# A decoder layer kernel: the gates' sigmoid by exponentials and logarithms, the suffix sums in two rounded passes

## The reference

```python
h = rms_norm(x, g_norm_mix[l]) * (1 + scale1) + shift1
proj = h @ w_in[l]                                  # q, k, v of both attention branches
...
# stick-breaking attention, 4 heads of 64
z = jnp.einsum('bqhd,bshd->bhqs', qb, kf) * scale
log_1m = jnp.where(mask, jax.nn.log_sigmoid(-z), 0.0)
suffix = lax.cumsum(log_1m, axis=3, reverse=True)
between = jnp.concatenate([suffix[..., 1:], jnp.zeros_like(suffix[..., :1])], axis=-1)
a = jnp.where(mask, jnp.exp(jax.nn.log_sigmoid(z) + between), 0.0)
...
g_dil, g_sb = jnp.split(jax.nn.sigmoid(h @ w_branch_gate[l]), 2, axis=-1)
merged = g_dil * (o_dil @ w_branch_dil[l]) + g_sb * (o_sb @ w_branch_sb[l])
x = x + gate1 * (merged @ w_out[l])
h2 = rms_norm(x, g_norm_ffn[l]) * (1 + scale2) + shift2
# 32 SwiGLU experts of width 512, two for each token; x + gate2 * y is the output
```

## Time and profile before

| | us |
|---|---|
| median of 3 runs | 959.87 |
| lowest and highest | 957.65, 960.79 |
| the profiled execution | 957.36 |
| its span in the profile | 955.6 |

### The profile page before, as it was taken

The page is one execution under the profiler, slowest core; times in us unless marked ns, Lnnn a source line. Parts: engine busy times, 40 slices in busy tenths (PEclk is TensorE's granted clock), DMA queues, the critical chain, the costliest instruction groups (busy, mean ns, idle before and its releaser), DMA issues.

```text
span 955.6 us, 11365 instructions
## 1 busy us (share of the span) xinstructions
PE 898.8 (94%) x4241; PEld 518.9 (54%) x4241; DVE 464.6 (49%) x829; ACT 197.5 (21%) x331; POOL 135.0 (14%) x168
## 2 busy tenths in 40 slices
PE   3989999999989999999899999999999999899897
PEld 2556779998867666488544443444344433333332
DVE  2441356538797766733663443344334424334224
ACT  3432233335433333403200000000000000000000
POOL 1000112302242111522101000000000000000000
PEclk9989999999999999999899999999999999999999
DMA  9966765240323203352889999999999999999995
GB/s 344 329 231 230 265 221 177 103 161 7 117 71 123 88 1 142 140 237 105 346 315 395 423 421 420 421 421 421 421 421 422 422 421 422 421 421 424 421 415 205
DMA packets 60077, 275.04 MB, mean 288 GB/s; under 512 B 8756, under 2 KB 21052, under 8 KB 31876
## 3 DMA queue, kind: packets, MB, share of 16 engines
q1 hardware_dynamic: 54772, 264.41, 69.3%
q0 software_dynamic: 3952, 9.19, 2.6%
q10 hardware_dynamic: 1312, 0.87, 0.4%
HBM read 263.71 MB, written 14.70 MB: 291 GB/s over the span
## 4 chain that ended last, share of the span: by engine, by line
PE 68%; SPq 19%; DMA 6%; DVE 3%; issue 2%; ACT 2%; DVEq 0%; ACTq 0%
PE ps L719 26%; PE ps L1093 14%; SPq L440 14%; PE ps L1112 7%; PE ps L1066 4%; DMA arena<-in_w_expert_down 3%; SPq L448 2%; PE ps L669 2%; PE ps L880 2%; SPq L395 2%; DMA arena<-in_w_ada 1%; PE ps L913 1%; PE ps L905 1%; PE ps L834 1%; DMA xn<-in_w_ada 1%
## 5 line engine op out<-in xcount | busy, mean ns | idle before, releaser
L1093 PE MATMUL ps<-arena,hT 128*64 128x512 f32 x1024 | 229.0, 596 | 5.0 <-DMA arena<-in_w_expert_up 4.4
L1093 PEld LDWEIGHTS ps<-arena,hT 128*64 128x64 f32 x1024 | 70.2, 137 | 146.7 <-issue 133.5
L1112 PE MATMUL ps<-arena,hT 128*64 128x512 f32 x512 | 116.9, 598 | 11.8 <-DMA arena<-in_w_expert_down 11.8
L1994 DVE TENSOR_SCALAR hT<-hT 128x256 f32<-128x256 f32 x32 | 9.4, 293 | 240.1 <-ACT hT L1472 240.1
L719 PE MATMUL ps<-slot_r,xs_r 128*128 128x512 f32 x320 | 106.2, 404 | 0.4 <-issue 0.4
L719 PE MATMUL ps<-xs_r,slot_r 128*128 128x512 f32 x320 | 101.8, 399 | 0.8 <-DVE hT_r L1574 0.5
L719 PE MATMUL ps<-slot_r,hT_r 128*128 128x512 f32 x224 | 88.1, 393 | 0.0
L719 PEld LDWEIGHTS ps<-slot_r,xs_r 128*128 128x128 f32 x320 | 77.3, 262 | 10.5 <-ACT arena L1332 2.5
L1112 PEld LDWEIGHTS ps<-arena,hT 128*64 128x64 f32 x512 | 33.9, 136 | 74.8 <-issue 59.6
L719 PEld LDWEIGHTS ps<-xs_r,slot_r 128*128 128x128 f32 x320 | 59.3, 190 | 16.7 <-issue 2.9
L635 POOL COPY idx<-small 128x1 int32 (+1 forms) x32 | 6.8, 212 | 414.4 <-DVE hT L2016 393.2
(11 more groups left out here) (297 smaller groups left out, 1078.1 us busy)
## 6 DMA issues: line engine op xcount, KB each, us to landing
arena<-in_w_expert_gate SPq DMA_DIRECT2D x64, 1024.0 KB, 24.5
arena<-in_w_expert_up SPq DMA_DIRECT2D x64, 1024.0 KB, 26.9
arena<-in_w_expert_down SPq DMA_DIRECT2D x32, 2048.0 KB, 29.6
xn<-in_w_ada SPq DMA_DIRECT2D x16, 1024.0 KB, 4.7
arena<-in_w_in SPq DMA_DIRECT2D x12, 1024.0 KB, 8.0
arena<-in_w_ada SPq DMA_DIRECT2D x8, 1024.0 KB, 14.6
arena<-in_w_branch_gate SPq DMA_DIRECT2D x4, 2048.0 KB, 8.1
xs<-in_x SPq DMA_DIRECT2D x8, 512.0 KB, 9.3
```

Source lines behind the costliest of these rows:

```text
L1093: mm = pe.matmul(ps[64 * h:64 * h + 64, 2, :], xeT[:, xb, k, CAP * j:CAP * (j + 1)], w_gu(b)[:, :, k, 256 * h:256 * h + 256], start=(k == ...
L1112: mm = pe.matmul(ps[64 * h:64 * h + 64, 4, :], hhT[:, f % 2, 64 * (f // 2):64 * (f // 2) + 64], w_dn(b)[:, f, h * CH:(h + 1) * CH], start= ...
```

## The change

The diff has five parts.

- Gates. Scalar takes log(1+exp(-|x|)) in three passes (`gate_log`: absolute value, exponential, logarithm), VectorE takes min(x,0) minus it out of the PSUM bank (`gate_finish`, which signals `gate_arg`), Scalar takes the exponential (`gate_close`). Gate products and branch products wait on `gate_arg` in place of `gate_exp`.
- Suffix sums. Softplus is split into a rounded part (Scalar, `split_sp`) and the rest (VectorE, `split_sp`), and the sums are 20 float32r matmuls in place of ten fp32 ones.
- adaLN. `ada_more` comes one unit later, `mod_round`, `columns` and the third bias load too.
- Tail. The two parts of x1 are first copied into natural order (Scalar, `natural`, eight copies into two free weight slots), `residual` reads them without a stride, and the middle of the last gate and up product waits for them (`hotT_ok` 5 in place of 3). `add_y` sums in place, and the output is stored from there.
- `ones` and `tri` get rounded copies, made by Scalar at the start; elsewhere `one` is the same memory as fp32.

```diff
+        ones_r = sb("ones_r", [P, P], F32R)
+        tri_r = sb("tri_r", [P, P], F32R)
...
+        sp_hi, sp_lo = (xn_r[:].rearrange("p t n -> p (t n)")[:, at:at + SB_COLS] for at in (1280, 2560))
+        one = ones_r[:].bitcast(F32)
...
-        x1n = arena[:, EXP_W:EXP_W + NT * D].rearrange("p (t n) -> p t n", t=NT)
+        x1_part = [slot_r[j][:].rearrange("p k n -> p (k n)").rearrange("p (t n) -> p t n", t=NT) for j in (3, 7)]
...
             for u in range(QK_FIRST, QK_LAST + 1):
                 m, t, ch = u - QK_FIRST, u % NT, u // NT
-                if m == 0:
+                if m == 1:
                     columns(0)
-                if m == KC + 1:
+                if m == KC + 2:
                     columns(1)
...
-            for u in range(2):
-                ada_more(u)
+            ada_more(0)
...
-                if u < 2 * KC:
-                    ada_more(u)
+                if u <= 2 * KC:
+                    ada_more(u - 1)
...
-                    pe.wait_ge(gate_exp, f)
+                    pe.wait_ge(gate_arg, f)
                 elif f >= 2:
-                    pe.wait_ge(gate_exp, f - 1)
+                    pe.wait_ge(gate_arg, f - 1)
...
                 b = 3 * (h % 2)
-                pe.wait_ge(sp_ok, h + 1)
-                for j in range(NT):
+                def sums(part, j):
                     for j2 in range(j, NT):
                         a = b * CH + SB_OFF[j] + (j2 - j) * P
-                        mm = pe.matmul(psf[:, a:a + SEQ - j2 * P], (tri if j2 == j else ones)[:],
-                                       sp_[:, SB_OFF[j2]:SB_OFF[j2] + SEQ - j2 * P],
-                                       start=(j2 == j), stop=(j2 == NT - 1), skip_group_check=True)
+                        mm = pe.matmul(psf[:, a:a + SEQ - j2 * P], (tri_r if j2 == j else ones_r)[:],
+                                       part[:, SB_OFF[j2]:SB_OFF[j2] + SEQ - j2 * P],
+                                       start=(part is sp_hi and j2 == j), stop=(part is sp_lo and j2 == NT - 1),
+                                       skip_group_check=True)
+                    return mm
+
+                pe.wait_ge(sphi_ok, h + 1)
+                for j in range(NT - 1):
+                    sums(sp_hi, j)
+                pe.wait_ge(sp_ok, 2 * h + 2)
+                for j in range(NT - 1):
+                    sums(sp_lo, j)
+                sums(sp_hi, NT - 1)
+                mm = sums(sp_lo, NT - 1)
                 mm.then_inc(sf_ps, 1)
 
...
-                    pe.wait_ge(gate_exp, 10)
+                    pe.wait_ge(gate_arg, 10)
                 elif f == 6:
-                    pe.wait_ge(gate_exp, 2 * KC)
+                    pe.wait_ge(gate_arg, 2 * KC)
...
-                            pe.wait_ge(hotT_ok, 3)
+                            pe.wait_ge(hotT_ok, 5)
...
                 for t, h in parts:
-                    bank = ps[:, final_bank(t, h), :].rearrange("p (c k) -> p c k", k=KC)
-                    for part in (xs_r, xn_r):
-                        pe.matmul(bank, ident_r[:], part[:, t, :].rearrange("p (k c) -> p c k", k=KC)[:, 64 * h:64 * h + 64, :],
-                                  start=(part is xs_r), stop=False, skip_group_check=True)
+                    for part in (0, 1):
+                        pe.matmul(ps[:, final_bank(t, h), :], ident_r[:], x1_part[part][:, t, h * CH:(h + 1) * CH],
+                                  start=(part == 0), stop=False, skip_group_check=True)
...
+            act.wait_ge(consts, 4)
+            act.activation(ones_r[:], ones[:], ACT.Copy).then_inc(consts, 1)
+            act.activation(tri_r[:], tri[:], ACT.Copy).then_inc(consts, 1)
...
-                if u == KC + 1:
+                if u == KC + 2:
...
-            def gate_exp_(f):
+            def gate_log(f):
+
                 act.wait_ge(gate_ps, f + 1)
-                act.activation(gT[:, f, :], ps[:, gate_bank(f), :], ACT.Exp, scale=-1.0).then_inc(gate_exp, 1)
+                g = gT[:, f, :]
+                link(act.activation(g, ps[:, gate_bank(f), :], ACT.Abs))
+                link(act.activation(g, g, ACT.Exp, scale=-1.0))
+                act.activation(g, g, ACT.Ln, bias=1.0).then_inc(gate_exp, 1)
+
+            def gate_close(f):
+                act.wait_ge(gate_arg, f + 1)
+                act.activation(gT[:, f, :], gT[:, f, :], ACT.Exp).then_inc(gate_ok, 1)
...
-                gate_exp_(s)
                 probs_store(s)
+                gate_log(s)
                 if s % NT in (1, 2):
                     split_hi(7 + s // NT, s % NT - 1)
                 if s >= NT + 1:
                     mix_exp(s - NT - 1)
-            gate_exp_(8)
+                if s >= 1:
+                    gate_close(s - 1)
             mix_exp(NT - 1)
+            gate_log(8)
 
...
+            def split_sp(h):
+                act.wait_ge(sp_ok, 2 * h + 1)
+                act.activation(sp_hi, sp_[:, 0:SB_COLS], ACT.Copy).then_inc(sphi_ok, 1)
 
...
-            gate_exp_(9)
+            gate_log(9)
+            split_sp(0)
+            gate_close(7)
+            gate_close(8)
             for h in range(NH):
                 if h == 0:
                     split_hi(9, 0)
                     split_hi(9, 1)
                 sb_exp(h)
+                if h == NH - 1:
+                    gate_close(15)
                 if h + 1 < NH:
                     sb_logs(h + 1)
-                    gate_exp_(10 + 2 * h)
+                    gate_log(10 + 2 * h)
+                    gate_close(9 + 2 * h)
+                    split_sp(h + 1)
+                sb_store(h)
                 if h in (1, 2):
                     split_hi(10, h - 1)
-                sb_store(h)
                 if h + 1 < NH:
-                    gate_exp_(11 + 2 * h)
+                    gate_log(11 + 2 * h)
+                    gate_close(10 + 2 * h)
...
+            def natural(part, src):
+
+                for t in range(NT):
+                    ins = act.activation(x1_part[part][:, t, :].rearrange("p (c k) -> p c k", k=KC),
+                                         src[:, t, :].bitcast(F32).rearrange("p (k c) -> p c k", k=KC), ACT.Copy)
+                ins.then_inc(hotT_ok, 1)
+
+            act.activation(ident_r[:], ident[:], ACT.Copy).then_inc(hotT_ok, 1)
+            natural(0, xs_r)
             sig(NE - 2)
-            act.activation(ident_r[:], ident[:], ACT.Copy).then_inc(hotT_ok, 1)
             for j in range(2):
                 act.wait_ge(last_ps, j + 1)
                 act.activation(hotT[:, j].rearrange("p t n -> p (t n)"), ps[:, 6 * j, :], ACT.Copy).then_inc(hotT_ok, 1)
+            natural(1, xn_r)
             sig(NE - 1)
 
             def act_round(rnd):
...
+                if u in (KC, 2 * KC):
+                    mod_round(u // KC)
...
-                if u == KC - 1:
-                    mod_round(1)
-                if u == 2 * KC - 1:
-                    mod_round(2)
-                if u == 2 * KC + 3:
+                if u == 2 * KC + 5:
...
                 dve.wait_ge(gate_exp, f + 1)
-                link(dve.tensor_scalar(gT[:, f, :], gT[:, f, :], 1.0, None, ALU.add))
-                dve.reciprocal(gT[:, f, :], gT[:, f, :]).then_inc(gate_ok, 1)
+                dve.scalar_tensor_tensor(out=gT[:, f, :], in0=ps[:, gate_bank(f), :], scalar=0.0, in1=gT[:, f, :],
+                                         op0=ALU.min, op1=ALU.subtract).then_inc(gate_arg, 1)
...
-                if s < 2 * NT - 1:
-                    gate_finish(s)
+                gate_finish(s)
...
+            def split_sp(h):
+                dve.wait_ge(sphi_ok, h + 1)
+                dve.tensor_tensor(sp_lo, sp_[:, 0:SB_COLS], sp_hi.bitcast(F32), ALU.subtract).then_inc(sp_ok, 1)
...
             sb_softplus(0)
+            split_sp(0)
             out_T(2)
             out_T(3)
-            gate_finish(2 * NT - 1)
+            gate_finish(8)
             for h in range(NH):
                 sb_args(h)
-                for f in (8, 9):
-                    gate_finish(2 * h + f)
+                gate_finish(9 + 2 * h)
                 if h < NH - 1:
                     dil_gate(2 * h)
                 if h + 1 < NH:
                     sb_copy(h + 1)
                     sb_softplus(h + 1)
+                    gate_finish(10 + 2 * h)
+                    split_sp(h + 1)
                     dil_gate(2 * h + 1)
             dil_gate(6)
             dil_gate(7)
...
-                step(dve.tensor_tensor(x1n[:, t, :], y_in[:, t, 0, :], y_in[:, t, 1, :], ALU.add))
+                step(dve.tensor_tensor(y_in[:, t, 0, :], y_in[:, t, 0, :], y_in[:, t, 1, :], ALU.add))
```

More of the change, by code:

```diff
@@ L84, in hybrid_layer @@
                 nc.sbuf_tensor("hT", [P, KC, SEQ], F32) as hT, \
-                nc.sbuf_tensor("xn", [P, NT, D], F32) as xn:
+                nc.sbuf_tensor("xn", [P, NT, D], F32) as xn, \
+                nc.sbuf_tensor("ones", [P, P], F32) as ones, \
+                nc.sbuf_tensor("tri", [P, P], F32) as tri:
             pass
```

(32 more changed lines are left out.)

2 lines of the change are left out of this document (1 added, 1 removed).

## The result

The changed kernel is slower, by more than forecast: a median of 984.57 us (981.09 to 986.57, four executions) against 958.76 (956.30 to 960.79) measured beside it. The ratio is 1.026, 95% interval 1.023 to 1.029. That is +25.8 us where the prediction had +13.5 and a range up to 981. The profiled execution took 981.09 us (span 979.3), 23.7 us more than before's.

The account below looks back on a forecast made before the run. TensorE's path outside the weight-streamed experts was taken as the bound. Terms -6.9 + 0 - 6.0 + 2.8 + 14.4 + 1.8 + 3.3 + 6.6 - 2.5 = +13.5 us gave 970.9 profiled, median 973.4, range 962 to 981.

Parts of the forecast that it names:

- the argument's place: Heads: TensorE waits for VectorE's gate argument, +14.4 us at gates 11, 13, 15, +1.8 at 12, 14, +3.3 at dil_product(6).
- Rival B: Heads: the argument is finished before the values end, so TensorE stays dense and the kernel takes 947.3 us; chance 0.08.
- A: Heads: the clock stays up through the new idles, so the kernel takes 966.8 us; chance 0.25.
- Clock: Heads: three new idles of 4.8 us each bring slow work of 2.2 us, +6.6 us, bounds 0 and 10.
- Tail: After the experts: natural-order residual matmuls save more than the wait for Scalar's copies costs, -2.5 us, at most 3.5.
- Suffix sums: Four heads: 20 rounded matmuls take 2.8 us for 4.33 of ten fp32 ones, -6.0 us, bounds 0 to 7.7.
- Start: Start of the projections: a transfer wait is hidden and the slow product and unit run at full clock, -6.9 us.
- Dilated stage: Dilated stage: Scalar's later copy frees one TensorE stall and catches the next, 0 us, bounds -4 to +2.
- Head 0: Ahead of head 0's sums: Scalar's gate 9 passes and rounding copy, then VectorE's subtraction, delay them, +2.8 us.
- rival C: Head 0: GpSimd holds VectorE's second mask addition, the branch product waits 4.6 us more, 978.0 or 984 us; chance 0.13.

Follow-up runs that it names:

- x3_tail: The changed kernel with the tail of before (no natural copies, strided residual, `hotT_ok` 3): 984.14 us.
- x5_maskps: x1_swap with the triangle mask put on the sums in PSUM ahead of VectorE's subtraction: 961.52 us, ratio 1.004 to the kernel before.
- x4_recip: The changed kernel without its gates part (one exponential on Scalar, add and reciprocal on VectorE): 953.99 us, ratio 0.994 to the kernel before.
- x6_shift: The kernel before with the adaLN part alone: 951.47 us, ratio 0.993.
- x9_recip_early: x4_recip with the natural copies of x1's second half behind expert 30's sigmoid, ahead of the hot transposes: 950.62 us, ratio 0.989 to the kernel before.
- x10_recip_fill: x9_recip_early with seven matmuls into an unused bank in the wait ahead of head 0's sums: 950.94 us.
- x11_recip_tail: x4_recip with the tail of before (no natural copies, strided residual): 951.07 us, ratio 0.990 to the kernel before.
- x1_swap: The changed kernel with gate_finish(10+2h) moved ahead of sb_copy(h+1) and sb_softplus(h+1) on VectorE: 971.56 us, ratio 1.012 to the kernel before.
- x2_fill: The changed kernel with 19 matmuls that nobody reads ahead of each of gates 11, 13 and 15: 980.67 us, ratio 1.0225 to the kernel before.
- x8_all: x5_maskps plus gate_finish(9+2h) ahead of sb_args(h), gate 9's passes behind split_sp(0), and earlier natural(1): 950.48 us, ratio 0.989 to the kernel before.
- x7_sums: The kernel before with the two-pass suffix sums alone: 958.03 us, ratio 0.998.

## Why the prediction missed

The direction and the mechanism were right: +14.4, +1.8 and +3.3 for the argument's place are 14.3, 1.6 and 3.1 in the trace. Rival B (dense heads) did not come true, and neither did A: the clock fell behind each of the three waits, here and in x3_tail. The gain of the sums was right too. The terms that missed lie on one side, and the profiled execution is 10.2 us above the sum of +13.5:

- **Clock, the step that failed most: +6.6, measured +10.7 in the heads and at the branch products.** Gates 11, 13 and 15 cost 2.9, 2.1 and 2.4 us more than 5.75, near the 2.2 forecast each (0.9 us over in sum). But gate 12, behind a wait of 0.84, took 7.31, and `dil_product(6)` and (7), behind 3.1, took 5.28 for 3.6: 3.2 us that the sum had at nothing. The prediction gave waits under 4.6 us nothing because the stall of 2.6 us in 268 to 271 had left the clock at 1.00. The runs contradict that in both directions: behind head 0's wait of 1.76 to 1.80 us the sums were slow in five of five profiled executions without a fill, behind 2.95 us in the three that are told above and in x5_maskps, but not in the changed kernel's; and the wait of 2.65 that left the clock alone before and in x4_recip was followed by slow transposes (1.84 to 1.97 us for 1.09) in x6_shift, x9_recip_early, x10_recip_fill and x11_recip_tail. The wait of 0.84 ahead of gate 12 was followed by a slow gate here, in x1_swap and in x2_fill, and not in x3_tail, nor one of 0.86 in x5_maskps. A wait alone, by its length, does not tell whether the clock falls; one execution per kernel shows one draw. The Trainium skill, "TensorE: Matmul & The Clock Gate", section "What's actually happening", says that the monitor behind the clock runs freely and does not start with the kernel, so that the same kernel changes level at another point in another run. The runs agree in that the outcome differs from run to run; that this is the cause, none of them shows.
- **Tail: -2.5, measured +1.7 in its stage.** The copies were priced at 1.05 us, the unstrided row, and take 1.93; only the term's lower value of 1.1 used VectorE's stride factor of 1.12/0.70, which gives 1.7 us a copy. And the wait of 4.6 us was itself an idle that lowers the clock, which the sum counted in the heads and forgot here. The `down` just ahead of the tail, 5.35 us for 3.65, is in the column before. It is not the change's doing by any run here: it stood behind a wait of 1.9 us that the kernel before has too, and it was slow in x3_tail and x9_recip_early and fast before, in x4_recip, x8_all and x11_recip_tail.
- **Suffix sums: -6.0, measured -6.2** (1.4 in head 0, 1.6 in each other head; 2.73 for 4.33 in the chain, 2.8 estimated). The gain was right with some luck: 20 sums take 3.2 us from start to start, more than the 2.8, and the other 0.4 came from starting that much sooner behind the branch product, which nobody had priced. And by x7_sums the part alone moves the median by 0.7, since head 0 gives most of it back.
- **Start: -6.9, measured -6.4**, and -7.3 as a median in x6_shift. The cause was read rightly: no wait and full clock at 52 us. The missing 0.5 is a wait of 0.54 us ahead of the second product, at 58.2: the transfer, taken as wholly hidden, was not quite.
- **Dilated stage: 0 with bounds -4 and +2, measured +0.9**, and +2.6 to +3.9 in five other profiled executions with this stage unchanged (x1, x2, x3, x5, x8): the wait moved and grew from 2.65 to 3.4 us, and mostly the clock fell behind it. The upper bound was too low.
- **Head 0: +2.8, measured +2.5** (z(0) to the sums 11.30 us for 8.81). What was priced as rival C at 0.13 happens in part: in three executions that leave head 0 alone TensorE waits 3.0 us ahead of `dil_product(0)`. That and the dilated stage are probably most of what lies between the profiled execution (981.1) and the slower ones (986.5 and 986.6).

The gaps: clock in the heads 4.1, tail 4.2, the last `down` 1.3 (the net of its column), dilated stage 0.9, start 0.5, the waits for the argument -0.5, head 0 -0.3, sums -0.2: 10.0 of the 10.2. The terms that rest on an order of instructions came out within 0.5 us, and those that rest on the clock or on a row of another access pattern were off by up to 4 us each. The range was drawn as if these errors were independent; one cause, the clock, stood behind most of them, and its upper bound of 10 us lies under the 10.7 of the heads alone.

What stays open: why the clock falls behind one wait of a given length and not behind another, and why the expert stage takes 515.7 to 520.7 us with the same work.

## What to carry to other kernels

When the last reader of a buffer moves from one engine to another, look at what stands in that engine's queue ahead of the reader, and for whom that itself waits; here one call moved up by two lines was worth 13 us. Freeing VectorE of 3.35 us per gate was worth nothing as long as TensorE waited for VectorE's queue, and 3.3 us in the heads once it did not. Price every new wait of TensorE twice, once for the idle and once for the slow work behind it, in every stage where one appears: behind 4.8 us the slow work came six times of six here, behind 0.75 to 0.86 us three times of nine, so a short wait gets a price with a chance and not nothing. A part that wins in three heads of four and loses in the first is worth measuring alone before it is stacked on others.

## What the runs showed of the hardware

- A Scalar copy of 128x1024 fp32 that rounds and reads with a stride took 1.91 to 2.01 us, the same without a stride 1.05.
- VectorE is held to within 0.5 us of the end of GpSimd's running subtraction in mask additions with two SBUF inputs (4.20 and 4.52 us for 0.56 and 0.29), and also in the addition of a constant with a single one (4.62 us for 0.42). The reciprocal behind it, SBUF to SBUF, ran at its usual 3.35 us beside GpSimd, and a subtraction of 1280 columns with one operand in PSUM at its usual 1.49. The Trainium skill, "SBUF — State Buffer", section "Who interferes with whom", which the prediction used for two-input operations, also counts tensor_scalar among those that can take the shared ports, if its operands meet conditions; the 4.62 us agrees.
- Rounded matmuls of 128 to 512 columns: 20 of them with 5120 columns together take 3.2 us (at a granted clock of 1.00), 0.62 ns a column, where 128x512 ones in a row take 0.24 us each, 0.46 ns a column.
- Matmuls whose result nobody reads kept the granted clock at 1.00 through waits of 1.8 and 4.8 us (sums of 3.2 us behind the first for 4.4 to 4.6, gates of 5.73 us behind the second for 7.8 to 8.6).
